# The feed-forward input products by Strassen's form on all but the first tile pairs, and VectorE in GpSimd's place for the Hyena filters

## The reference, cut to what matters

```python
def conv_ffn(h, w_up, conv_w, w_down):            # D_FF = 2816: w_up is 1024 x 5632
    a, g = jnp.split(dwconv(h @ w_up, conv_w), 2, axis=-1)
    return (jax.nn.silu(g) * a) @ w_down

def hyena_filters(n, w1, b1, w2, b2, w3, freq):
    ...
    h = (h @ w3.astype(f32)).reshape(n, HY_ORDER, 2, HY_CH)     # two sides of a filter
    h = h * jnp.exp(-t[:, None, None, None] * deltas)
    kern = jnp.concatenate([h[:, :, 0], jnp.zeros((1, HY_ORDER, HY_CH), f32), jnp.flip(h[1:, :, 1], axis=0)], axis=0)
    kern = kern * lax.rsqrt(jnp.sum(kern * kern, axis=0, keepdims=True) + EPS)
    return jnp.fft.rfft(kern, axis=0)

def hyena(u, conv_w, kf, bias):
    v, x1, x2 = jnp.split(dwconv(u, conv_w), 3, axis=-1)
    z = v
    for o, gate in enumerate((x1, x2)):
        z = gate * (fft_long_conv(z, kf[:, o]) + z * bias[o])    # spectrum of z times kf
    return z
```

## Time and profile before

| | |
|---|---|
| median of 3 runs | 2585.8 us |
| the profiled execution | 2582.52 us, its span 2580.7 us |
| mean granted TensorE clock | 0.961 |
| PE busy | 2352.9 us (91%) |
| DVE busy | 879.0 us (34%) |
| ACT, POOL busy | 544.5 us (21%), 318.5 us (12%) |

### The profile page before, as it was taken

The page is one execution under the profiler, slowest core; times in us unless marked ns, Lnnn a source line. Parts: engine busy times, 40 slices in busy tenths (PEclk is TensorE's granted clock), DMA queues, the critical chain, the costliest instruction groups (busy, mean ns, idle before and its releaser), DMA issues. The chain is left out here.

```text
span 2580.7 us, 37602 instructions
## 1 busy us (share of the span) xinstructions
PE 2352.9 (91%) x16466; PEld 1615.4 (63%) x16466; DVE 879.0 (34%) x1653; ACT 544.5 (21%) x1266; POOL 318.5 (12%) x363
## 2 busy tenths in 40 slices
PE   4999899979966999999999999898887799999998
PEld 1556655558855755555558999544543584444798
DVE  2125722277641422222220003333666532222111
ACT  2103622321202311111110012111551131111111
POOL 1000100047630000000001000000563200000000
PEclk9999899989987999999999999998898899999999
DMA  8341011000021212121205557411000222222354
GB/s 315 131 163 34 1 33 33 1 2 4 4 82 52 66 33 66 33 66 33 66 25 153 162 165 209 138 49 45 1 1 17 65 66 86 77 66 87 90 148 133
DMA packets 190534, 193.46 MB, mean 75 GB/s; under 512 B 4691, under 2 KB 174370, under 8 KB 190178
## 3 DMA queue, kind: packets, MB, share of 16 engines
q1 hardware_dynamic: 177506, 145.53, 18.6%
q0 software_dynamic: 11776, 42.27, 4.5%
q10 hardware_dynamic: 1088, 3.26, 0.4%
HBM read 188.94 MB, written 2.10 MB: 74 GB/s over the span
## 5 line engine op out<-in xcount | busy, mean ns | idle before, releaser
L1442 PE MATMUL banks<-mem 128*128 128x512 f32 x1312 | 618.1, 591 | 0.0
L1776 PE MATMUL banks<-mem 128*128 128x128 f32 x3520 | 403.5, 276 | 11.4 <-PEq L1365 9.9
L1776 PEld LDWEIGHTS banks<-mem 128*128 128x128 f32 x3520 | 398.8, 193 | 21.4 <-issue 20.1
L1442 PEld LDWEIGHTS banks<-mem 128*128 128x128 f32 x1312 | 247.8, 189 | 171.9 <-issue 153.2
L362 DVE SCALAR_TENSOR_TENSOR mem<-banks,mem 128x511 f32<-128x511 f32 (+1 forms) x168 | 106.1, 660 | 702.8 <-ACT mem L1513 325.3
L1445 PEld LDWEIGHTS banks<-mem 128*128 128x128 f32 x672 | 127.1, 189 | 161.9 <-issue 161.9
L1445 PE MATMUL banks<-mem 128*128 128x256 f32 x672 | 200.1, 378 | 0.0
L1861 PE MATMUL banks<-mem 128*128 128x512 f32 x400 | 190.8, 608 | 6.0 <-issue 6.0
L1511 ACT ACTIVATE mem<-banks,mem 128x512 f32<-128x512 f32 x88 | 60.7, 689 | 626.6 <-PE banks L1445 373.5
L1387 PE MATMUL banks<-mem 128*128 128x256 f32 x640 | 143.3, 384 | 14.5 <-PEq L616 11.1
L921 PE MATMUL banks<-mem 64*64 64x64 f32 x3840 | 127.8, 220 | 18.5 <-DVE mem L1197 11.4
(11 more groups left out here) (330 smaller groups left out, 2693.9 us busy)
## 6 DMA issues: line engine op xcount, KB each, us to landing
mem<-in_ffn_w_up SPq DMA_DIRECT2D x44, 1024.0 KB, 5.5
mem<-in_ffn_w_down SPq DMA_DIRECT2D x64, 704.0 KB, 6.5
mem<-in_w_mod POOLq DMA_DIRECT2D x40, 1024.0 KB, 7.4
mem<-in_ab_w_in SPq DMA_DIRECT2D x14, 1024.0 KB, 5.3
mem<-in_w_mod SPq DMA_DIRECT2D x8, 1024.0 KB, 14.1
mem<-in_cd_w_in SPq DMA_DIRECT2D x8, 1024.0 KB, 5.3
mem<-in_ab_w_out SPq DMA_DIRECT2D x4, 1024.0 KB, 9.2
mem<-in_cd_w_out SPq DMA_DIRECT2D x4, 1024.0 KB, 9.1
```

The source lines that it names most:

```text
L1442: last = nc.tensor.matmul(c.ps[:, bank, :], w[:, k, :], ht[:, k, 0:N_X], start=k == 0, stop=k == KT - 1)
L1776: last = c.nc.tensor.matmul(c.ps[:, n % self.n_banks, 0:128], hidden[:, k, t * 128:(t + 1) * 128], w, start=k == 0, stop=k == FT - 1)
```

## The change

In all pairs but the first (layer 0) or the first two (layer 1), the value and gate tile are one 2x2 product: the weights are split by tile and by half of the 1024 inputs, the tokens by half of the inputs and half of the tokens. It is done by the Winograd variant of Strassen's form: seven products of four matmuls each, over 384 columns (layer 0) or 256 (layer 1), instead of eight. DVE makes the joined weights (4 sums of 128x512 per pair, kept in the slots' free halves and over the weights), the joined tokens once per layer (4 sums), and adds the products up (7 sums per pair) into rows in the SBUF, which ACT and the convolution then read. ACT has one more copy per pair. A ring slot now holds one tile of 512 KB; a pair takes two slots, and the next pair's load into them starts when all seven products are done. The eight banks go round among the products. The gate buffer has one place instead of two.

In the filters, POOL first joins the sides of `w3` (sum and difference; one small correction for the zero lag), PE multiplies by the joined columns, DVE multiplies by the decay out of the bank, and POOL is left with the sums of squares. DVE also does the spectrum steps' sum and difference. In `convolutions` all spectrum products are DVE's, 1024 elements at a time.

```diff
@@ plan_all
     def up(w):
-        both = chunks(w)
-        return [both[i] for j in range(11) for i in (j, 11 + j)]
+        both = chunks(w, 128)
+        return [both[i] for n in range(FT) for i in (n, FT + n)]
@@ mix_and_up, SP and PE
+            over = lambda n: (up_product, 2 * n + 2) if n < begun else (strassen, 7 * (n - begun + 1))
+            c.issue(sp, f"up{l}", lambda j: over(j // 2), earlier=first_up)
...
+                def times(name, weights, tokens):
+                    q = 7 * i + fast.ORDER.index(name)
+                    if q >= 8:
+                        owner, of = fast.ORDER[(q - 8) % 7], (q - 8) // 7
+                        if owner == "p1":
+                            pe.wait_ge(copied, of + 1)
+                        else:
+                            pe.wait_ge(whole, 7 * of + fast.FREED[owner])
+                    elif q in (4, 6):
+                        pe.wait_ge(convolved, begun if q == 4 else 2 * begun)
+                    for k in range(4):
+                        last = nc.tensor.matmul(fast.out(i, name), weights[:, k, :], tokens[:, k, :], start=k == 0, stop=k == 3)
+                    last.then_inc(strassen, 1)
...
+                times("p1", gate_w[:, 0:4], fast.b11)
+                times("p2", gate_w[:, 4:8], fast.b21)
+                pe.wait_ge(tokens_joined, 2)
+                pe.wait_ge(weights_joined, 4 * i + 2)
+                times("p6", s2, fast.t2)
+                times("p5", s1, fast.t1)
+                pe.wait_ge(tokens_joined, 4)
+                pe.wait_ge(weights_joined, 4 * i + 4)
+                times("p7", value_w[:, 0:4], fast.t3)
+                times("p3", s4, fast.b22)
+                times("p4", value_w[:, 4:8], fast.t4)
@@ mix_and_up, DVE
+            for n in range(begun, FT):
...
+                if n + 1 < FT:
+                    join_weights(n + 1)
+                if i:
+                    convolve_pair(n - 1, 0)
+                    convolve_pair(n - 1, 1)
+                dve.wait_ge(copied, i + 1)
+                add_up(i, gate_rows[1], gate_rows[0], "p6")
+                add_up(i, gate_rows[0], gate_rows[0], "p2")
+                multiply(n - 1)
...
+                add_up(i, gate_rows[1], gate_rows[1], "p3")
+                add_up(i, value_rows[0], value_rows[0], "p4")
@@ Filters
+    def join_sides(self, pool):
+        hy, g = self.hy, self.c.nc.gpsimd
+        pool.wait_ge(self.came, self.LOADED)
...
     def multiply(self, pe, n, part):
...
         if n == 0 and part == 0:
-            pe.wait_ge(self.came, self.LOADED)
+            pe.wait_ge(self.joined, self.JOINED)
...
-    def weigh(self, pool, n):
+    def weigh(self, dve, n, part):
...
+            self.c.nc.vector.tensor_tensor(hy.lags[:, part, t, :], self.c.ps[:, self.banks[part], :], hy.decay[:, t, :],
+                                           ALU.mult).then_inc(self.ready, 1)
@@ attention_and_filters, DVE
                 if i < n_pairs:
                     maximum(2 * i)
                     maximum(2 * i + 1)
+                if 0 <= i - 2:
+                    filters.unfold(dve, i - 2)
+                if 0 <= i - 1 < n_pairs:
+                    filters.weigh(dve, i - 1, 0)
+                if i < n_pairs:
                     weigh(2 * i)
+                if 0 <= i - 1 < n_pairs:
+                    filters.weigh(dve, i - 1, 1)
+                if i < n_pairs:
                     weigh(2 * i + 1)
@@ convolutions, DVE
-                for mirror, total in enumerate((one, other)):
-                    v.tensor_tensor(total, z(0, mirror), kern(0, mirror), ALU.mult)
-                    link(v.tensor_tensor(part, z(1, mirror), kern(1, mirror), ALU.mult))
-                    link(v.tensor_tensor(total, total, part, ALU.subtract))
+                v.tensor_tensor(sums, hy.z[0], kern(0), ALU.mult)
+                link(v.tensor_tensor(parts, hy.z[1], kern(1), ALU.mult))
+                link(v.tensor_tensor(sums, sums, parts, ALU.subtract))
+                v.tensor_tensor(sums_s, hy.z[0], kern(1), ALU.mult)
+                link(v.tensor_tensor(parts, hy.z[1], kern(0), ALU.mult))
+                last = v.tensor_tensor(sums_s, sums_s, parts, ALU.add)
```

More of the change, by code:

```diff
@@ L1401, in up @@
             def up(n, half, tokens):
[L1402 to L1403 removed]
+                w = fast.weights(n, half)
                 bank = 4 * (n % 2) + 2 * half
@@ L1501, in gate, with middle @@
                 act.wait_ge(convolved, 2 * n + 2)
-                f(gbuf[:, n % 2, 0:n_all], gbuf[:, n % 2, 0:n_all], ACT.Silu).then_inc(gated, 1)
-            for n in range(FT):
+                f(gbuf[:, 0:n_all], gbuf[:, 0:n_all], ACT.Silu).then_inc(gated, 1)
+            def middle(n, half):
+                act.wait_ge(whole, 7 * (n - begun) + 6 + half)
+                if half:
+                    act.wait_ge(done, n)
+                elif n > begun:
+                    act.wait_ge(convolved, 2 * (n - 1) + 1)
+                dst = gbuf if half else hidden[:, n, :]
+                f(dst[:, 0:n_all], fast.raw(n, half), ACT.Identity, scale=middle_tap(n, half)).then_inc(drained, 1)
+            for n in range(begun):
                 for half in range(2):
@@ new lines, in add_up, with convolve_pair @@
+            def add_up(i, to, one, name):
+                dve.wait_ge(strassen, 7 * i + fast.ORDER.index(name) + 1)
+                v.tensor_tensor(to, one, fast.out(i, name), ALU.add).then_inc(whole, 1)
+            def convolve_pair(n, half):
+                dve.wait_ge(drained, per * 2 * begun + 2 * (n - begun) + half + 1)
+                raw = fast.raw(n, half)
+                convolve(c, link, gbuf if half else hidden[:, n, :], raw, raw[:, N_X:n_all], z,
+                         lambda t: ffn_tap(c, l, t, n + half * FT)).then_inc(convolved, 1)
@@ L1580, in _ @@
+            join_tokens()
+            for n in range(begun):
+                if n == begun - 1:
+                    join_weights(begun)
+                    join_tokens_in_place()
                 for half in range(2):
@@ L2718, in multiply @@
         last.then_inc(self.product, 1)
-    def place(self, n, part):
+    def weigh(self, dve, n, part):
         hy = self.hy
-        if self.lag_step(n)[1]:
-            return hy.lag_raw[2 * (n % 2) + part]
-        f, s = (n % 8 - 4) // 2, n % 2
-        return hy.kern[n // 8][:, s, f] if part == 0 else hy.lag_raw[2 * (n % 2) + 1]
-    def keep(self, act, n):
-        c = self.c
-        lags_before, lag = self.lag_step(n)
-        for part in range(2):
-            act.wait_ge(self.product, 2 * n + part + 1)
-            if n >= 2 and part == 0:
-                self.after(act, n - 2)
-            scale = c.tab["nonzero"] if lag and part and n % 8 == 0 else 1.0
-            c.nc.scalar.activation(self.place(n, part), c.ps[:, self.banks[part], :], ACT.Copy, scale=scale)\
-                .then_inc(self.kept, 1)
@@ L2740, in after @@
-    def after(self, eng, n):
-        lags, lag = self.lag_step(n)
-        if lag:
-            eng.wait_ge(self.ready, 2 * (lags + 1))
-            eng.wait_ge(self.squared, 2 * (lags + 1))
-        else:
-            eng.wait_ge(self.unfolded, 2 * (4 * (n // 8) + n % 8 - 4 + 1))
+        if self.is_lag(n):
+            order, t = n // 8, n % 8
+            if n == 0 and part == 0:
+                dve.wait_ge(self.came, self.LOADED)
+            dve.wait_ge(self.product, 2 * n + part + 1)
+            self.c.nc.vector.tensor_tensor(hy.lags[:, part, t, :], self.c.ps[:, self.banks[part], :], hy.decay[:, t, :],
+                                           ALU.mult).then_inc(self.ready, 1)
@@ L3002, in convolutions @@
     u = cd_buffers(c)[7]
-    z = lambda s, mirror: hy.tmp[2 * s + mirror]
+    z = lambda s, mirror: hy.z[s][:, mirror]
+    sums, parts, sums_s = hy.products
     bank = lambda order, f: 4 * ((order + f) % 2)
-    one, part, other = hy.tmp[4:7]
-    one_s, part_s, other_s, other_part_s = hy.tmp[7:11]
     def tokens_of(k, t):
```

266 lines of the change are left out of this document (167 added, 99 removed).

## The result

| | before | after |
|---|---|---|
| median of the runs timed together (4 each) | 2583.14 us | 2485.55 us (2484.33 to 2486.57) |
| the profiled execution, its span | 2582.52, 2580.7 us | 2486.43, 2484.6 us |
| mean granted clock | 0.961 | 0.961 |

The ratio is 0.9622, interval 0.9606 to 0.9638: 97.6 us less. The forecast was 2478 us, its range 2460 to 2506.

A forecast was written before the change was run, and what follows sets the result against it. PE's columns were taken to bound up, chains through DVE and POOL the Hyena stages. -84.1 - 9.6 - 13 = -106.7 us from 2582.5 gives 2475.8; with the runs' median 3.3 above, 2478 us was predicted, range 2460 to 2506.

The forecast's parts named there:

- Up, -84.1: Both up parts: seven products of four save 87.4 us if PE never waits, less 3.3 us for longer tails.
- rival 1: Up, layer 1: VectorE is the bound, its operations at 1.3 times their price; 2511 us, chance 0.12.
- rival 3: Up: weights come too late, PE waits in layer 1 above an arrival of 8.9 us; slower, chance 0.03.
- A: Up: time from a pair's start until the next pair's two 512 KB weight loads land, taken as 5.6 us.
- rival 4: Up: weight loads are not hidden behind matmuls, layer 1 loses 91 us; 2537 us, chance 0.02.
- The convolutions, -9.6: Convolutions: DVE's products before PE's start take 10.0 us, 2.4 less in each of four passes; between -13 and 0.
- Attention and filters, -13: Attention and filters: 27 us of POOL's hold-ups go, 14.4 us of new costs come; between -22 and +6.
- the 27: Attention and filters: us expected to go, of some 30 excess, with POOL down from six operations per lag step to two.
- +5 us: Filters: POOL's joins of `w3` delay PE's first filter product from 1801.66 to 1804.8 or later; at least 0, at most 12.
- +4: Attention and filters: DVE has 1.3 us more per lag step, making `weigh` and the next maximum 0.5 us later, eight times.
- Rival 2: Hyena stages give nothing back: slow joins, DVE late for the exponentials, -13 becomes +6; 2497 us, chance 0.15.
- 6 us for loading code: Filters, POOL: a skill rule's cost for a freshly loaded kernel's first call, about 6 us; left out of the sum.

The follow-up runs named there:

- e8: Changed kernel, with the first half of each up part's last pair convolved before the last sum (product p4); 2484.76 us.
- e4: Changed kernel, with SP starting the load for the next pair three products of PE later than the ring allows; 2527.55 us.
- e3: Changed kernel, with SP starting the load for the next pair one product of PE later than the ring allows; 2482.97 us.
- e6: Changed kernel, with DVE's unfolding moved ahead of the maxima and its copy of the finished values right behind them; 2470.29 us.
- e7: Changed kernel, with POOL's joins of w3 waiting for w3's own load and no longer for all five filter tables; 2476.65 us.

## Why the prediction was right, and where its terms were off

1. *Up, -84.1: right.* The pairs were to give 54.0 and 33.4 us, and gave 54.9 and 32.5 in twelve of the thirteen executions. The gaps grew by 1.62 and 1.06 us, for 2.0 and 1.3. Together -84.7. The shape that the trace of before had, 256 columns at 1.685 ns, carried this term.
2. *Its reason for the gap was wrong in part.* It had both halves' taps follow the last matmul, "as the last half can't be convolved before the first". But the first half need not wait: e8 convolves it ahead of the last sum. The size held all the same, since that order exposes a second drain.
3. *DVE is no bound (rival 1).* Predicted 9.4 and 12.3 us per pair, busy 8.6 and 11.4. The taps kept their price out of the SBUF (in columns as the earlier trace rows), and DVE was idle ahead of each join, for 3.2 us where some 2 were foretold (busy us, mean ns | idle before it):

```profile
L366 DVE SCALAR_TENSOR_TENSOR mem<-mem 128x511 f32<-128x511 f32 x38 | 28.5, 751 | 1.3
...
L1639 DVE TENSOR_TENSOR mem<-mem 128x512 f32<-128x512 f32 x20 | 13.9, 694 | 64.5 <-DMA mem<-in_ffn_w_up 64.5
```

4. *The weights come in time (rival 3), but not by much.* The chain was right and A was 0.5 us too small; e4 shows the rival's mechanism at work when A grows by 5.2.
5. *Weight loads are hidden (rival 4 fell).* In layer 1 they are busy for 211.72 us inside 242.0 us of unbroken matmuls. The rule of the Trainium skill (TensorE: Matmul & The Clock Gate, The mechanism) that they overlap only when their row groups differ would have them bare, and is contradicted; the same section also allows for a background weight buffer, and with that the trace agrees.
6. *The convolutions, -9.6: right.* From DVE's first product to PE's start:

```profile
1896.25 1.23 DVE L3288 TENSOR_TENSOR mem<-mem 128x1024 f32<-128x1024 f32 x1
...
1905.38 0.69 DVE L3301 TENSOR_TENSOR mem<-mem 128x512 f32<-128x512 f32 x1
```

   PE starts at 1906.21, 9.96 us on, for the predicted 10.0; the earlier trace rows had 12.46. The stage fell by 9.1, and by 12.6 in the executions with more clock.
7. *Attention and filters, -13: mis-sized.* It was -4.0 in the profiled execution, and -2.0 to -9.9 over the five executions of this attention code. The rest of this point is the profiled one. The iterations that POOL held up (the 5th, 6th, 13th and 14th from the stage's start) gave 21.2 us of the 27, and the rest grew by 17.2 instead of 14.4.
   - The step that failed was the cost of the joins and the added products, "+5 us" and "+1". Iteration 2 alone grew by 6.5 us: 3.2 of wait ahead of the first filter product, and 3.3 for its two added matmuls, at a clock of 0.50. The next two iterations grew by 3.9 more, at the lower clock. "PE stands still there, and slower after" named that and gave it no price of its own.
   - "+4" for DVE's added work was near by luck. Iterations 7 to 12 grew by 4.6, but 2.7 of it lies in 7 to 9. These are spectrum steps, in which PE waits for the sum and difference that DVE took over (L2916), and for them the prediction had no price. The lag steps 10 to 12, for which it had one, grew by 1.9.
   - The 5.8 us of the 27 that did not come lie in iterations 5 and 14, 9.55 and 10.55 us long. e3 did them in 8.17 and 8.92 with the same code, which is the clock; e6 in 6.80 and 6.78, which is the clock and the waits for L3151.
   - Rival 2 came half true by its own signs: iterations took 8.15 us, over its 7.5, and the wait ahead of the first filter product was 3.2 us, under its 6.
8. *No 6 us for loading code.* The reload stands between the memory clears and the first small operation. In e7 that operation starts at 1740.88, 0.1 us behind the clears' end, and the joins run at 1.26 us each. Nor do the 6 us hide ahead of the clears: `w3` was issued at 1735.1 and landed 5.3 us later, and they start at 1740.44. By the Trainium skill (GPSIMD Engine Reference, Instruction dispatch) the first call behind the reload was to pay some 6 us; no row here shows them.
9. *What was in no term.* The work ahead of up in layer 0 ended 3.0 us earlier, the work from down of layer 0 to attention took 2.2 more and the norm ahead of up in layer 1 1.7 more. Over all executions these move both ways on unchanged code.

The sum, stage by stage: -84.7 - 4.0 - 9.1, -3.0, +2.2 + 1.7, +0.8 in the last down part: -96.1, the spans' difference. The forecast sum was -106.7: of the 10.6 us between them attention has 9.0, the convolutions 0.5, up -0.6, and 1.7 is in no term. The forecast itself is only 7.6 us off, since before's median came out 2.7 us lower than the one it was set on. That the total came so near is owed to up, whose 84.7 us are seven eighths of it: the two Hyena stages together gave 13.1 us of 22.6.

Four slips in the working moved nothing of note. 2475.8 + 3.3 is 2479.1, and not 2478. "-55 with layer 1 at its old 13.74 us" is -54.0, or -50.7 with the tails. By the prediction's own terms layer 0 waits above A = 14.7, and not 14.9. And rival 1 at 1.3 times the prices costs 20 x 0.13 = 2.6 us; for its 33 us a pair would have to take 13.74 us and not 12.2.

## What to carry to other kernels

Trading PE's work for VectorE's pays in full where PE has no gap and the trace has the new shape; work out the one chain that frees the next bank, from the transfer's start on, as it tells the slack to a fraction of a microsecond. In a stage of chained waits, put no price on an engine's load but on each wait, and give the clock behind a wait a price of its own. Where PE waits at the head of such a stage, see whether anything can run in the wait: here 40 useless matmuls gave 10 us, and the three edits to the waits 16 together.
